# One order instead of another: products of a half-chunk with the weights' high parts first, then those with the low parts

## The reference, cut to what matters

```python
q, k, v, g = jnp.split(h @ w_in, 4, axis=-1)                 # 2048 x 8192
...
return (o * jax.nn.silu(g)) @ w_out                          # 2048 x 2048
...
return x + (p_i @ w_pp) * jax.nn.sigmoid(x @ w_pg)           # 2048 x 2048
...
f = (jax.nn.silu(hn @ w_gate[l]) * (hn @ w_up[l])) @ w_down[l]   # 2048 x 5632, twice; 5632 x 2048
```

## Time and profile before

| | |
|---|---|
| median of the runs | 2170.02 us (2169.51 to 2170.37) |
| the profiled execution | 2173.58 us |
| its span, first to last instruction | 2171.8 us |
| mean granted TensorE clock | 0.999 of full speed |
| TensorE busy | 2156.8 us (99%), 12000 matmul records |
| VectorE busy | 1391.3 us (64%) |
| ScalarE busy | 1155.8 us (53%) |
| DMA | 393.77 MB, 181 GB/s in the mean |

### The profile page before, as it was taken

How to read it: one execution, slowest core, us unless ns; L and a number is a source line. 1 busy time by engine, 2 the same in 40 slices (tenths; PEclk the granted TensorE clock), 3 DMA queues, 4 the chain that set the end, 5 groups by cost and what they waited for, 6 DMA issues and landing times.

```text
span 2171.8 us, 29214 instructions
## 1 busy us (share of the span) xinstructions
PE 2156.8 (99%) x12000; PEld 1866.3 (86%) x12000; DVE 1391.3 (64%) x1745; ACT 1155.8 (53%) x1529; POOL 27.8 (1%) x42
## 2 busy tenths in 40 slices
PE   9999999999999999999999999999999999999998
PEld 8888888888888888888888888888888888888887
DVE  6665555657787666577657787576656544565655
ACT  6555454555766565566545555565445444444443
POOL 1000000000010000000000000000000000000000
PEclk9999999999999999999999999999999999999999
DMA  7566666565656454566665555556666666666654
GB/s 246 172 185 174 183 171 179 169 190 179 192 161 182 137 155 151 184 200 189 189 182 167 171 169 183 186 164 186 193 187 192 191 193 192 190 192 187 208 184 150
DMA packets 223124, 393.77 MB, mean 181 GB/s; under 512 B 20905, under 2 KB 42930, under 8 KB 222864
## 3 DMA queue, kind: packets, MB, share of 16 engines
q1 hardware_dynamic: 221664, 388.35, 59.9%
q0 software_dynamic: 1184, 3.50, 0.5%
q10 hardware_dynamic: 144, 0.07, 0.0%
HBM read 389.76 MB, written 2.11 MB: 180 GB/s over the span
## 4 chain that ended last, share of the span: by engine, by line
PE 94%; DVE 4%; ACT 1%; issue 0%; DMA 0%; SPq 0%; DVEq 0%; ACTq 0%
PE ps L904 93%; DVE WL L1450 1%; PE ps L914 1%; DVE TMP L1450 0%; DVE xT L1450 0%; DVE H L1453 0%; DVE O L1453 0%; DMA XN<-in_x 0%; ACT WH L1181 0%; ACT SQ L1181 0%; ACT KEPT L1194 0%; DVE gT L1453 0%; ACT L1185 0%; ACT gT L1181 0%; DVE gT L1450 0%
## 5 line engine op out<-in xcount | busy, mean ns | idle before, releaser
L1450 DVE TENSOR_TENSOR WL<-RAW,WH 128x1024 fp32r<-128x1024 f32 (+1 forms) x733 | 887.6, 1222 | 425.5 <-ACT WH L1181 423.1
L1181 ACT ACTIVATE WH<-RAW 128x1024 fp32r<-128x1024 f32 (+1 forms) x733 | 768.4, 1055 | 664.6 <-PE ps L904 656.2
L904 PE MATMUL ps<-H,WH 128*128 128x512 f32 x3157 | 1113.4, 397 | 1.3 <-DVE WL L1450 0.6
L904 PE MATMUL ps<-H,WL 128*128 128x256 f32 x3152 | 882.3, 280 | 0.0
L904 PEld LDWEIGHTS ps<-H,WH 128*128 128x128 f32 x3157 | 591.7, 188 | 138.5 <-DVE WL L1450 2.1
L904 PEld LDWEIGHTS ps<-H,WL 128*128 128x128 f32 x3152 | 595.7, 189 | 1.4
L904 PE MATMUL ps<-O,WH 128*128 128x512 f32 (+2 forms) x1383 | 476.3, 392 | 2.1 <-DVE WL L1450 2.0
L904 PE MATMUL ps<-O,WL 128*128 128x256 f32 x1344 | 375.9, 280 | 0.0
L904 PEld LDWEIGHTS ps<-O,WH 128*128 128x128 f32 x1383 | 256.8, 188 | 60.7 <-DVE WL L1450 3.1
L904 PEld LDWEIGHTS ps<-O,WL 128*128 128x128 f32 x1344 | 253.7, 189 | 0.4
L904 PE MATMUL ps<-WH,ACTS 128*128 128x512 f32 x704 | 218.3, 390 | 0.0
(11 more groups left out here) (225 smaller groups left out, 1358.3 us busy)
## 6 DMA issues: line engine op xcount, KB each, us to landing
RAW<-in_w_in_a SPq DMA_DIRECT2D x127, 512.0 KB, 3.7
RAW<-in_w_in SPq DMA_DIRECT2D x96, 512.0 KB, 3.6
RAW<-in_w_gate SPq DMA_DIRECT2D x88, 512.0 KB, 3.9
RAW<-in_w_up SPq DMA_DIRECT2D x88, 512.0 KB, 3.9
RAW<-in_w_down SPq DMA_DIRECT2D x88, 512.0 KB, 4.8
RAW<-in_w_ple_gate SPq DMA_DIRECT2D x64, 512.0 KB, 3.8
RAW<-in_w_in_b SPq DMA_DIRECT2D x40, 512.0 KB, 3.7
RAW<-in_w_out_a SPq DMA_DIRECT2D x32, 512.0 KB, 3.6
```

Of the source, the lines that this page charges most:

```text
L904: return e.matmul(o, l, r, start=start, stop=True, skip_group_check=True)
L1181: return e.activation(o, i, f, **kw)
L1450: return e.tensor_tensor(o, x, y, op)
```

## The change

In an ordinary group's half-chunk the H matmuls of all four weight blocks are issued first, then their four L matmuls in the same order (HHHHLLLL where it was HLHLHLHL). The list `held` keeps the weight blocks whose L is still to be issued; `lows()` issues them when at least TOGETHER = 4 are held or the half ends. The events go with the L of the same weight block as before. Natural, solo and one groups and the first chunk of fg0 are left as they are, and so are the waits at the head of a chunk. The number and the operands of the matmuls are the same.

```diff
+TOGETHER = 4
...
-                for j, t in order[part * len(order) // 2:(part + 1) * len(order) // 2]:
+                held = []
+
+                def lows():
+
+                    for j, t in held:
+                        b, k = g.banks[t], ks[j]
+                        m = mm(ps[:, b, S:2 * S], lo[:, j, t * P:(t + 1) * P], g.xs[:, k, 0:S])
+                        marked(m, j, t)
+                    held.clear()
+
+                def marked(m, j, t):
+                    end = j == js[-1] and t == g.nt - 1
+                    whole = last and j == js[-1] and (g.solo or t % 2 == 1 or end)
+                    names = ([("full", name, t if g.solo else t // 2)] if whole else []) + ([("used", i)] if end else [])
+                    if names:
+                        m.then_inc(*ev(dense_done, *names))
+
+                items = order[part * len(order) // 2:(part + 1) * len(order) // 2]
+                for n_, (j, t) in enumerate(items):
                     b, k = g.banks[t // 2 if g.one else t], ks[j]
...
                     else:
                         mm(ps[:, b, :], wh, g.xs[:, k, :], first and j == 0)
-                        m = mm(ps[:, b, S:2 * S], wl, g.xs[:, k, 0:S])
-                    end = j == js[-1] and t == g.nt - 1
-                    whole = last and j == js[-1] and (g.solo or t % 2 == 1 or end)
-                    names = ([("full", name, t if g.solo else t // 2)] if whole else []) + ([("used", i)] if end else [])
-                    if names:
-                        m.then_inc(*ev(dense_done, *names))
+                        held.append((j, t))
+                        if n_ >= TOGETHER - 1 or n_ == len(items) - 1:
+                            lows()
+                        continue
+                    marked(m, j, t)
```

## The result

| | before | changed |
|---|---|---|
| median | 2170.16 us (2169.51 to 2170.37) | 2179.71 us (2179.34 to 2180.10) |
| ratio | | 1.0044, 95% interval 1.0033 to 1.0054 |
| profiled execution, its span | 2173.58 us, 2171.8 us | 2179.34 us, 2177.5 us |

The change makes the kernel slower by 9.6 us. The time lies in the predicted range, but on the other side of no change than the forecast of 2164 us; it is where the third rival put it (2179 to 2185 us).

What follows compares the result with a forecast made beforehand. The prediction took TensorE's start-to-start pace as the bound: -9.2 us of slips plus 2.9 us of restarts gave -6.3 us, so 2167.3 us profiled and, with the median 3.56 us lower, 2164 us; range 2159 to 2181.

Steps and rivals of the forecast that it cites:

- the third rival: Additional 384-column matmuls no longer heal slips; about 2260 clean pairs slip: 2185 us, or 2179 at 4 ns; chance 0.24.
- What bounds the kernel, and the two paces: TensorE, busy 99% of the span, never waits to speak of; an HL pair takes 0.3466 us clean, 0.3534 slipping.
- No new waits: Waits for activations, banks and low parts add 0; TensorE's idle time before the H, 3.4 us, bounds it.
- The clean half of the new order, 1387 ns: HHHHLLLL half-chunk, summed from one-width streams: 1387 ns against 1386 clean before, +1 ns x 1156 = 1.2 us.
- I take it that four H in a row let the stream settle: In each half-chunk, four H end the slipping as five or six do elsewhere, so the 9.2 us go.
- The old slips vanish, -9.2 us: 57 slow stretches, 478.54 us in all, lose 9.2 us to slipping pairs; the new order removes this.
- some 95 restarts of 0.03 us: After scores, turn, pv, rotations and other work, each restart still costs 0.02 to 0.04 us: 2.9 us in all.
- the second rival: Slips stay as they are, as the new order has as many H to slip: 2170 us (2167 to 2173); chance 0.32.

Runs made afterwards that it cites:

- the runs with equal widths: Changed kernel with every L over 512 columns: 2651.01 us; changed kernel with every H issued as two matmuls of 256 columns: 2220.70 us.
- the second trace: The kernel before, unchanged, run and profiled once more: 2171.61 us, ratio 0.9999.
- the run with eight: Changed kernel with a chunk's L held to its end: 2184.64 us; with L after each half in a group's last chunk: 2176.72 us.

## Why the prediction failed

- **What bounds the kernel, and the two paces**: right. TensorE sets the end in every run here, and a pair takes 346.6 or 353.4 ns. That the additional matmuls of 384 columns end a slow stretch was read from one place and holds for the sum: without them 2183.22 us, as computed for that run from the same numbers. It doesn't hold at each of the twelve places, and a stretch can be clean without one, too: the pairs from 117 to 126 us are, and the first of these matmuls stands at 424.
- **No new waits**: right, 3.2 us of idle time before the H instead of 3.4.
- **The clean half of the new order, 1387 ns**: here it failed. The sum was put together from streams of one width: L after L in a group with nothing but 256 columns, H after H in a natural group. Each of these is clean by itself, as the runs with equal widths show once more, but HHHHLLLL isn't: 1403.3 ns. The term was taken as +1 ns and is +16.9 ns a half. The one place of the trace with the new pattern showed 0.94 us from four H to the next L, with 0.91 clean; I put the difference down to a late start of the first H alone. For that trace this is right (the single steps are 256, 227, 227 and 230 ns), but in the second trace the same four steps are 269, 240, 229 and 236 ns. The row was one outcome of two, it stood behind other work and lasted one round, so it couldn't tell the pace of a stream.
- **"I take it that four H in a row let the stream settle"**: the step on which the sign hung. In the run with eight, a chunk loses 20 ns whereas two halves of four lose 34, and its H are clean from the sixth on: that bears out that a longer run of H settles, but four don't suffice, and each run of L sets the stream off again. The prediction named this against its own forecast and gave it too little weight: natural groups need six matmuls of 512 columns, and the order offers four.
- **The old slips vanish, -9.2 us**: they did, as HLHL stretches; but every half of the new order slips 16.9 ns instead of 27 in some and 0 in most. The 2.9 us for some 95 restarts of 0.03 us was never measured by itself.
- **Third rival, the additional matmuls no longer heal**: right in direction, and right in that they heal nothing in the new order, as their removal there shows. That its 2179 is the measured time is luck: it let 2260 pairs slip by 4 ns on top of the old slips, where all 4624 slip by 4.2 and the old slips are gone. Its mechanism is too narrow: no stretch was found with clean halves in a row that they could have set up. The mixed pattern itself slips.
- **A pace that depends on the columns alone** would have given no change, as in the second rival. The Trainium skill (TensorE: Matmul & The Clock Gate, Back-to-back issue gap) gives N / 2.4 + 2.5 ns for an isolated matmul of N columns at the high clock and a sustained 131 ns for 512 columns in a stream with weight loads, and has no term for the order of widths. The runs agree with neither figure (227 ns for 512 columns, 120 for 256), and order counts: the same matmuls take 2170.97, 2179.71 and 2184.64 us (of which 8 are a wait for banks) in runs of two, four and eight.

What makes an H some ns longer isn't settled. Shown is that the loss in a steady stream needs both widths in it and doesn't depend on the weight buffer, nor on the sequence of banks, as the same sequence is clean with equal widths. The loss for a return from L to H is 0 or 6.8 ns with runs of one, 3.4 with two, 16.9 with four and 20 with eight, the last spread over the first five H. No view of the profile names its cause.

## What to carry to other kernels

When TensorE is the bound, read the pace of its stream from start to start, in places far apart, before any thought is given to the number of instructions: the same instructions can have more than one pace. Don't sum a mixed stream from streams of one kind; find the very pattern in a steady stretch and in more than one trace, or run it. Where matmuls of two widths mix, short runs (one or two) lost least here, and a matmul that computes nothing can be worth its time if it brings a stream into step.

## What the runs showed of the hardware

The step from one fp32r matmul to the next was 227 ns with 512 columns and 120 with 256 at a granted clock of 1.00, in streams of one width once they had settled. In slipping streams the H had 237 ns in the mean in HLHL (a fixed rhythm of 236, 233 and 241), 233 in HHLL and 232 in HHHHLLLL, while the L kept 115 to 119. HLHL has a clean rhythm (230 and 117 ns) and a slipping one, both of which last for tens of microseconds. What runs just before bears on which: a single matmul of 384 columns between two stretches moved it from the second to the first in most places, and the same code isn't in the same rhythm in every execution. HHLL had one pace only, in all places looked at. Holding the L of a chunk back to its end cost 8 us by the banks alone.
